# Two masked parts of the inverse levels made one block earlier, and the HGRN state decay put first in the levels' block

## What is computed

```python
def step(s, inp):                       # RWKV-7, one token after the other
    r_t, w_t, k_t, v_t, kk_t, a_t = inp
    sa = jnp.einsum('bhvk,bhk->bhv', s, -kk_t)
    s = (s * w_t[:, :, None, :] + sa[..., None] * (kk_t * a_t)[:, :, None, :]
         + v_t[..., None] * k_t[:, :, None, :])
    return s, jnp.einsum('bhvk,bhk->bhv', s, r_t)
...
s = s * jnp.exp(g_end)[..., None] + jnp.einsum(     # HGRN2, the state of a chunk
    'bshk,bshv->bhkv', kc * jnp.exp(g_end[:, None] - gcum), vc)
```

## Time and profile before

| | us |
|---|---|
| runs of the kernel before | 2561.02, 2562.30, 2566.64 (median 2562.3) |
| the profiled execution | 2559.03 |
| its span, from first to last instruction | 2557.2 |
| block of transposes, first to last instruction of DVE | 188.12 to 197.89 |
| block of levels, SP's issue to the last update of DVE | 198.14 to 269.28 |

### The profile page before, as it was taken

How to read it: one execution, slowest core, us unless ns; L and a number is a source line. 1 busy time by engine, 2 the same in 40 slices (tenths; PEclk the granted TensorE clock), 3 DMA queues, 4 the chain that set the end, 5 groups by cost and what they waited for, 6 DMA issues and landing times. The chain is left out here.

```text
span 2557.2 us, 46359 instructions
## 1 busy us (share of the span) xinstructions
PE 2337.9 (91%) x19032; PEld 2228.6 (87%) x19032; DVE 1707.3 (67%) x2774; ACT 1110.5 (43%) x1878; POOL 1666.3 (65%) x716
## 2 busy tenths in 40 slices
PE   5977856999999999999969976789999999999998
PEld 5957855999999999999969832779999999999997
DVE  4776463596677458888859264348867762888887
ACT  4512223445554444444436422334555544444443
POOL 4704005687666788888857644757866668888885
PEclk8978887999999999999989987889999999999999
DMA  4410003455444455555535542434544445555553
GB/s 154 152 48 34 34 9 107 139 175 169 146 143 147 158 182 181 182 181 182 182 106 165 187 148 84 130 124 157 182 149 142 148 143 182 182 180 182 181 182 124
DMA packets 101650, 369.68 MB, mean 145 GB/s; under 512 B 15328, under 2 KB 15680, under 8 KB 98112
## 3 DMA queue, kind: packets, MB, share of 16 engines
q1 hardware_dynamic: 101440, 366.71, 43.1%
HBM read 352.08 MB, written 14.58 MB: 143 GB/s over the span
## 5 line engine op out<-in xcount | busy, mean ns | idle before, releaser
L274 POOL TENSOR_TENSOR weights_halves<-weights_raw,weights_halves 128x1024 fp32r<-128x1024 f32 x638 | 1540.2, 2417 | 586.0 <-ACT weights_halves L266 585.5
L266 ACT CAST weights_halves<-weights_raw 128x1024 fp32r<-128x1024 f32 x638 | 670.0, 1051 | 944.4 <-PE peer L295 480.8
L779 DVE TENSOR_TENSOR gated<-acts,gated 128x264 fp32r<-128x264 f32 x256 | 615.8, 2407 | 127.1 <-ACT gated L669 127.1
L295 PE MATMUL peer<-ffn_in_hi,weights_halves 128*128 128x264 f32 x4608 | 645.7, 288 | 19.5 <-PEq L162 19.5
L295 PEld LDWEIGHTS peer<-ffn_in_hi,weights_halves 128*128 128x128 f32 x4608 | 588.8, 189 | 23.6 <-issue 23.6
L283 PE MATMUL peer<-gated,weights_halves 128*128 128x264 f32 x2048 | 583.2, 285 | 0.0
L281 PE MATMUL peer<-gated,weights_halves 128*128 128x264 f32 x2048 | 581.3, 284 | 0.0
L282 PE MATMUL peer<-gated,weights_halves 128*128 128x264 f32 x2048 | 579.8, 283 | 0.0
L282 PEld LDWEIGHTS peer<-gated,weights_halves 128*128 128x128 f32 x2048 | 385.9, 188 | 0.0
L281 PEld LDWEIGHTS peer<-gated,weights_halves 128*128 128x128 f32 x2048 | 385.4, 188 | 0.0
L283 PEld LDWEIGHTS peer<-gated,weights_halves 128*128 128x128 f32 x2048 | 384.3, 188 | 0.0
(11 more groups left out here) (460 smaller groups left out, 2373.7 us busy)
## 6 DMA issues: line engine op xcount, KB each, us to landing
weights_raw<-in_up SPq DMA_DIRECT2D x256, 512.0 KB, 3.5
weights_raw<-in_down SPq DMA_DIRECT2D x256, 512.0 KB, 3.5
weights_raw<-in_ssm_w_in SPq DMA_DIRECT2D x40, 512.0 KB, 3.5
weights_raw<-in_w_q SPq DMA_DIRECT2D x32, 512.0 KB, 3.5
weights_raw<-in_ab_w_in SPq DMA_DIRECT2D x30, 512.0 KB, 3.4
weights_raw<-in_ssm_w_out SPq DMA_DIRECT2D x16, 512.0 KB, 3.9
states<-in_ssm_in SPq DMA_DIRECT2D x8, 1024.0 KB, 6.9
ssm_sample<-states SPq DMA_DIRECT2D x8, 1024.0 KB, 4.6
```

The costliest lines, as they stand in the source:

```text
L266: act.copy(self.halves[:, 0, slot, :], self.raw[:, slot, :]).then_inc(self.hi_made, 1)
L274: pool.tensor_tensor(self.halves[:, 1, slot, :], self.raw[:, slot, :], self.halves[:, 0, slot, :].bitcast(F32), ALU.subtract).then_inc(sel ...
L295: ins = pe.matmul(out, self.halves[:, half, n % RING, at], both[side], start=start and half == 0 and side == 0 and k == 0, stop=stop and h ...
L779: core.gated_lo.inc(dve.tensor_tensor(a_lo[:, j % RING, :], acts[:, j, :], a_hi[:, j % RING, :].bitcast(F32), ALU.subtract))
```

## The change

POOL's multiplies for the parts of levels 0 and 1 move from the block of levels to the block of transposes, where POOL had no program. In the block of levels POOL's first instruction is now the wait for the loaded states and their decay; the loop goes over levels 2 to 4 only. PE waits for a part only from level 2 on. `part` is handed to both functions. Nothing is computed otherwise.

```diff
--- before.py
+++ after.py
@@ -1243,7 +1243,7 @@
     return [(hp, tile, half) for hp in range(2) for tile in range(RWKV_TILES) for half in range(HALVES)]
 
 
-def turn_operands(core, par, mask, w, p, quad, lower, tu, toks, bound, key):
+def turn_operands(core, par, mask, w, p, quad, lower, tu, toks, bound, key, part):
 
     nc = core.nc
     stored = core.stored.at
@@ -1278,6 +1278,13 @@
                 act.wait_ge(sem("forget_made"), past("forget_made", 1))
                 act.activation(key, gate_f, ACT.Identity, bias=core.ones[:, 0:1], scale=-1.0)
 
+            @block.gpsimd
+            def _(pool):
+                for level in range(2):
+                    pool.tensor_tensor(part[:, level], quad[:, :, 0, :],
+                                       mask[:, MASK_LEVEL + 1 + level:MASK_LEVEL + 2 + level, :].broadcast_to((P, 16, P)),
+                                       ALU.mult)
+
             @block.vector
             def _(dve):
                 link = Link(dve, core.dve_done)
@@ -1298,10 +1305,9 @@
 SPREADS = 8
 
 
-def rwkv_levels(core, mask, quad, lower, tu, out, p, key, logf, logs, added, states, state_in, state_out):
+def rwkv_levels(core, mask, quad, lower, tu, part, out, p, key, logf, logs, added, states, state_in, state_out):
 
     nc = core.nc
-    part = core.ring.scratch()[:, 0:4096].rearrange("p (l c j) -> p l c j", l=2, c=16)
     product = lower.rearrange("p (g a) j -> p g (a j)", g=4)
     levels = 5
     values, q, forget = p[:, 22:26, SEQ:T], p[:, 14:18, SEQ:T], p[:, 18:22, :]
@@ -1322,17 +1328,14 @@
 
             @block.gpsimd
             def _(pool):
-                for level in range(levels):
-                    if level >= 2:
-                        pool.wait_ge(sem("first_made"), past("first_made", 4 * (level - 1)))
+                core.wait_loads(pool)
+                inc("states_decayed", pool.tensor_tensor(
+                    states, states, forget[:, :, SEQ:T].unsqueeze(3).broadcast_to((P, HGRN_TILES, DEC, P)), ALU.mult))
+                for level in range(2, levels):
+                    pool.wait_ge(sem("first_made"), past("first_made", 4 * (level - 1)))
                     inc("part_made", pool.tensor_tensor(
                         part[:, level % 2], quad[:, :, 0, :],
                         mask[:, MASK_LEVEL + 1 + level:MASK_LEVEL + 2 + level, :].broadcast_to((P, 16, P)), ALU.mult))
-                    if level == 1:
-                        core.wait_loads(pool)
-                        inc("states_decayed", pool.tensor_tensor(
-                            states, states, forget[:, :, SEQ:T].unsqueeze(3).broadcast_to((P, HGRN_TILES, DEC, P)),
-                            ALU.mult))
 
             @block.tensor
             def _(pe):
@@ -1346,7 +1349,8 @@
                     inc("spread_made", last)
 
                 for level in range(levels):
-                    pe.wait_ge(sem("part_made"), past("part_made", level + 1))
+                    if level >= 2:
+                        pe.wait_ge(sem("part_made"), past("part_made", level - 1))
                     for g in range(4):
                         n = 4 * level + g
                         if level:
@@ -1782,12 +1786,13 @@
                            (Room(tu.rearrange("p c a j -> p (c a j)")), toks_room, spare, spare),
                            d["rwkv_in"], d["rwkv_sample"], lambda act: hgrn_activations(act, p))
                 key = p[:, 4:8, :]
-                turn_operands(core, par, mask, w, p, quad, lower, tu, toks, bound, key)
+                part = scratch[:, 0:4096].rearrange("p (l c j) -> p l c j", l=2, c=16)
+                turn_operands(core, par, mask, w, p, quad, lower, tu, toks, bound, key, part)
                 room = Room(w_room)
                 states = room.take([P, HGRN_TILES, DEC, P])
                 logs = room.take([P, HGRN_TILES, SEQ])
                 added = whole(8, 4)[:, 0:1024].rearrange("p (n b v) -> p n b v", n=2, b=4)
-                rwkv_levels(core, mask, quad, lower, tu, out, p, key, p[:, 0:4, 0:SEQ], logs, added, states, d["hgrn_in"],
+                rwkv_levels(core, mask, quad, lower, tu, part, out, p, key, p[:, 0:4, 0:SEQ], logs, added, states, d["hgrn_in"],
                             d["hgrn_sample"])
                 gap = [whole(8, 4)[:, 0:1024].rearrange("p (t n) -> p t n", t=HGRN_TILES),
                        ups.rearrange("p a n -> p (a n)").rearrange("p (t n) -> p t n", t=HGRN_TILES)]
```

## The result

| | median us | runs | ratio to the kernel before, 95% interval |
|---|---|---|---|
| before | 2563.0 | 2561.02 to 2566.64 | |
| changed | 2579.6 | 2574.75 to 2581.18 | 1.0062 [1.0048, 1.0075] |
| changed, second series (median of 4) | 2577.8 | 2573.41 to 2580.95 | 1.0066 [1.0046, 1.0087] |

The forecast was 2571.0 us with a range of 2566 to 2575: the sign was right, and the time lies above the range. The profiled execution took 2574.75 us, its span is 2573.0, 15.8 more than the 2557.2 of the earlier trace rows.

A forecast was written before the change was run, and what follows sets the result against it. The prediction took DVE to bound the block of transposes and PE the block of levels; 8.7 - 4.5 + 3.0 + 1.5 = +8.7 us on the 2562.3 median gave 2571.0 us, range 2566 to 2575.

The forecast's parts named there:

- A: Block of transposes: DVE's large two-operand instructions take turns with POOL's two multiplies, +8.7 us (8.4 to 9.2).
- B: Start of the block of levels: PE no longer waits for part 0, -4.5 us (-4.6 to -4.3).
- C: Level 0 and first products of level 1: scans wait for POOL and PE stalls, +3.0 us (2.4 to 3.6).
- D: Behind PE's new stall in level 1: a low clock stretch falls on PE's path, +1.5 us (0.5 to 2.5).
- Rival (2): Block of transposes and level 0: POOL runs beside DVE without loss, -7.4 us, 2554.9; chance 0.07.
- rival (1): Block of levels: DVE's second scan gets through before part 2, sum +4.2, 2566.5 us; chance 0.13.
- the room of 1.2 us: Level 0: the maximum (L1416) gets through ahead of the decay with some 1.2 us of room, in about 0.7 us.
- T + 6.15: Level 0: the first addition was expected 6.15 us behind T, PE's start in the block of levels.
- Rival (3): Level 0: states land early, the maximum waits for the decay, PE stalls twice; about +11, 2573.5 us; chance 0.08.
- reaches the end whole: End of the two serial blocks: everything later hangs on it, so a microsecond won or lost there reaches the kernel's end.
- The lower bounds of the four terms: Lower bounds of A, B, C and D: 8.4, -4.6, 2.4 and 0.5; the prediction gave their sum as +7.0.
- the 21 us set against 12.8: Block of levels before the change: level 0 and level 1's first products took 21 us, the same work a level later 12.8.

The follow-up runs named there:

- one_part: Changed kernel with only part 0 made in the block of transposes, part 1 back in the block of levels; 2564.8 us, 1.0012.
- parts_set: Changed kernel with POOL setting the two parts to zero, four times each, instead of multiplying in the block of transposes; 2575.5 us, 1.0045.
- part0_by_dve: Kernel before, with DVE making part 0 in the block of transposes and the scans behind additions 15 and 23; 2553.2 us, 0.9958.
- scans_late: Changed kernel with DVE's four scans moved from behind additions 5 and 6 to behind 15 and 23; 2566.3 us, 1.0014.

## Why the prediction was wrong

Held against its own terms, in the order of its sum, from the first trace of each kernel:

| term | forecast | measured | from |
|---|---|---|---|
| A, block of transposes | +8.7 | +8.7 | DVE 186.81 to 205.24 = 18.43, before 9.77 |
| B, PE's wait for part 0 | -4.5 | -4.5 | PE 0.05 behind SP's load (205.54, 205.49), before 4.58 |
| C, level 0 and the stall in level 1 | +3.0 | +3.5 | PE goes on 23.36 behind its start, before 19.88 |
| D, clock behind the stall | +1.5 | +2.9 | from there to level 2 12.82, before 9.93 |
| two blocks | +8.7 | +10.5 | |
| the stages behind | 0 | +5.3 | 15.8 less 10.5; +5.6 in the two places, the rest before and behind them |

**Right:** that DVE and POOL take turns and that a DVE instruction with two SBUF operands stands aside for the whole of a POOL multiply. Term A is that, and one_part (4.4 us for one multiply), parts_set (0 for writes) and part0_by_dve (2.2 for DVE's own multiply) show it from three sides. Term B as well. The order of the turns was left open in the forecast, and it came out so that DVE got in twice behind the first multiply, with the tiny instruction and L1293; the sum is the same. Rival (2), POOL beside DVE without loss, is out; rival (1), both scans in one turn, too: the second waited for part 2. The new wait that took the place of the old is PE's 7.07 us for addition 7, and scans_late takes it away.

**Mis-sized, C:** the room of 1.2 us for the maximum ahead of the decay was nearly used up. PE's first products ran at the lower clock for longer (6.46 us for 32, 5.22 before), so the first addition came at T + 7.4 and not at T + 6.15; the maximum began at 213.54, the decay at 213.62, in its shadow, and ended 7.50 instead of 7.03 us later. That is the half microsecond. Rival (3) missed coming true by 0.08 us, and not by an early landing (8.1 us again) but by a late PE.

**Mis-sized, D:** I took the loss behind a short stall as a fixed 1.5 us. The low stretch was longer: all of 228 to 235 was granted at 0.50.

```profile
228.00:235.00 7.00, 6.10 (x28) 6.10 (x29) 2.11 (x4) 0.58 (x1) 3.94 (x1) 0.50 0.00 0
```

Before, the 4 us behind the stall of 2.93 us were at 0.57. A wait more than twice as long cost nearly twice as much behind it.

**The step that failed** is the first one: that a microsecond won or lost in these blocks "reaches the end whole", by which the stages behind stood in the sum at nothing. They cost 5.3 of the 15.8 us. No work hides at the end of the blocks, that was right; but the stages behind don't take the same time whenever they start. In the changed kernel PE's clock fell at two waits where it hadn't before (+2.9 and +2.7 us). Over all kernels of the study the first place moved by -4.6 to +3.0 us, by the clock, and the second by -3.9 to +2.7, by the clock where it rose above +2 and by the turns of DVE and POOL where it fell. The range had no term for it; with a plain one of some 5 us either way it would just have held the time. C and D alone, 1.9 us too low, would have stayed inside it.

**Two slips of the working** that change little. The lower bounds of the four terms add up to +6.7 and not +7.0. And the 21 us set against 12.8 are a level and the first products of the next; level 0 alone took 17.0 (202.72 to 219.75). Neither enters the forecast.

## What to carry to other kernels

Ahead of giving an idle GpSimd some work, look at what VectorE does in that stretch: in this kernel, beside instructions with two SBUF operands, a multiply on POOL cost DVE its whole length (4.4 us each here, more than the 2.2 us that DVE takes for it), beside instructions that read one operand from PSUM it was free (0.69 us with and without). Move POOL's work to such a stretch, or move the sensitive DVE instructions to where POOL has no queue; both together shortened the two blocks by 9.2 us here, of which moving the multiply gave some 4. And where the timing of a kernel with many short TensorE waits is forecast, let the range have room for clock steps and other turns far away from the change, and judge an edit by its own stretch in the trace as well as by the total.

## What the runs showed of the hardware

- When both engines have work queued, one POOL instruction and one DVE instruction go in turns, but the tiny DVE instruction did not use a turn up: L1292 (4 elements) and L1293 (2.28 us) both got in between POOL's two multiplies (11.10 us for the two; 8.97 with DVE idle). In the levels the scans of 0.7 us got one each: 8.49 us for two.
- A scan (TENSOR_TENSOR_SCAN with its operands in SBUF) and a TENSOR_SCALAR on 1024 elements collide like a two-operand multiply. The additions and maskings that read PSUM don't (0.69 us beside POOL's work as without it), and POOL's sets hold up nothing of DVE's large work.
- Where the clock falls is repeatable: between two traces of a kernel the stage up to 375 us differed by less than 0.1 us, between kernels by up to 7.6, with its granted clock between 0.78 and 0.85.
